# Block work of a normed token pair in another order, tiles turned one by one, scalings and weight blocks reordered at the kernel's start

## The reference

```python
x = x + 0.5 * swiglu(rmsnorm(x, norm_ffn1), w_ffn1_gate, w_ffn1_up, w_ffn1_down)
x = x + hybrid_mixer(rmsnorm(x, norm_mix), ...)      # windowed attention + gated linear attention
x = x + 0.5 * swiglu(rmsnorm(x, norm_ffn2), w_ffn2_gate, w_ffn2_up, w_ffn2_down)
return rmsnorm(x, norm_final)
# rmsnorm(x, g) = x * rsqrt(mean(x*x) + 1e-6) * g
# swiglu(h, wg, wu, wd) = (silu(h @ wg) * (h @ wu)) @ wd,   d_ff = 2816
```

## Time and profile before

| | us |
|---|---|
| median of three runs | 2178.97 (2178.81 to 2180.24) |
| the profiled execution | 2179.86 |
| its span | 2178.1 |
| TensorE busy (matmul) | 2140.5 |
| VectorE busy | 1500.4 |
| ScalarE busy | 842.4 |
| GpSimd busy | 330.0 |

### The profile page before, as it was taken

How to read it: one execution, slowest core, us unless ns; L and a number is a source line. 1 busy time by engine, 2 the same in 40 slices (tenths; PEclk the granted TensorE clock), 3 DMA queues, 4 the chain that set the end, 5 groups by cost and what they waited for, 6 DMA issues and landing times.

```text
span 2178.1 us, 32746 instructions
## 1 busy us (share of the span) xinstructions
PE 2140.5 (98%) x11950; PEld 1921.7 (88%) x11950; DVE 1500.4 (69%) x2702; ACT 842.4 (39%) x1688; POOL 330.0 (15%) x325
## 2 busy tenths in 40 slices
PE   6999999999999999999999999999999999999998
PEld 5999999999888888888888888899999999988887
DVE  7666677677666686988754557777776667757676
ACT  7233222222343355855543324422222322333343
POOL 7111111111100002201002334211111111100000
PEclk8999999999999999999999999999999999999999
DMA  4322222232586565433255872223322222387554
GB/s 127 101 82 91 91 88 88 97 106 91 186 287 208 174 209 163 132 103 108 79 150 167 285 240 95 65 88 97 100 97 82 91 91 87 113 285 256 176 187 166
DMA packets 245987, 301.17 MB, mean 138 GB/s; under 512 B 24194, under 2 KB 159746, under 8 KB 245828
## 3 DMA queue, kind: packets, MB, share of 16 engines
q1 hardware_dynamic: 237188, 285.97, 40.9%
q10 hardware_dynamic: 8640, 13.11, 1.7%
HBM read 206.29 MB, written 88.47 MB: 135 GB/s over the span
## 4 chain that ended last, share of the span: by engine, by line
PE 93%; DVE 3%; ACT 1%; issue 1%; DMA 1%; SPq 0%; POOL 0%; ACTq 0%; POOLq 0%; DVEq 0%
PE ps L2450 16%; PE ps L2446 12%; PE ps L2448 10%; PE ps L2449 10%; PE ps L2459 8%; PE ps L2458 8%; PE ps L2460 8%; PE ps L2372 4%; PE ps L2374 3%; PE ps L2373 3%; PE ps L2390 1%; PE ps L2392 1%; PE ps L2391 1%; PE ps L2643 1%; PE ps L2617 1%
## 5 line engine op out<-in xcount | busy, mean ns | idle before, releaser
L2450 PE MATMUL ps<-hs,w_lo 128*128 128x384 f32 (+1 forms) x992 | 305.2, 308 | 0.0
L2458 PE MATMUL ps<-w_hi,dh 128*128 128x512 f32 x770 | 300.2, 390 | 0.0
L2460 PE MATMUL ps<-w_hi,dh 128*128 128x512 f32 x770 | 299.7, 389 | 0.0
L1932 DVE TENSOR_TENSOR dh<-dr,dh 128x640 fp32r<-128x640 f32 x154 | 126.8, 823 | 161.7 <-ACT dh L1342 161.6
L2459 PE MATMUL ps<-w_lo,dh 128*128 128x512 f32 x610 | 237.3, 389 | 0.0
L2448 PE MATMUL ps<-hs,w_hi 128*128 128x384 f32 (+1 forms) x644 | 215.0, 334 | 4.9 <-DVE hs L1781 4.0
L1342 ACT CAST dh<-dr 128x640 fp32r<-128x640 f32 x154 | 112.2, 728 | 269.3 <-PE ps L2460 252.8
L2449 PE MATMUL ps<-hs,w_hi 128*128 128x384 f32 (+1 forms) x644 | 214.2, 333 | 0.0
L2446 PE MATMUL ps<-hs_first,w_hi 128*128 128x512 f32 x588 | 210.2, 391 | 0.0
L2446 PE MATMUL ps<-hs,w_hi 128*128 128x512 f32 x588 | 210.2, 391 | 0.0
L2449 PE MATMUL ps<-hq,w_hi 128*128 128x384 f32 x616 | 205.8, 334 | 0.0
(11 more groups left out here) (317 smaller groups left out, 4829.4 us busy)
## 6 DMA issues: line engine op xcount, KB each, us to landing
dr<-hid_mid SPq DMA_DIRECT2D x154, 320.0 KB, 3.2
w_raw<-in_w_ffn_down SPq DMA_DIRECT2D x176, 256.0 KB, 3.5
hid_mid<-st SPq DMA_DIRECT2D x88, 320.0 KB, 4.5
w_raw<-in_w_ffn_gate SPq DMA_DIRECT2D x44, 512.0 KB, 4.1
w_raw<-in_w_ffn_up SPq DMA_DIRECT2D x44, 512.0 KB, 3.9
hid_mid<-sg SPq DMA_DIRECT2D x66, 320.0 KB, 2.2
hq<-o_mid SPq DMA_DIRECT2D x70, 128.0 KB, 3.4
w_raw<-in_w_in SPq DMA_DIRECT2D x14, 512.0 KB, 5.5
```

The costliest lines, as they stand in the source:

```text
L1932: v.tensor_tensor(a_lo, DR[f][n % D_HID][:, :], a_hi.bitcast(F32), ALU.subtract).then_inc(W["a_lo"], 1)
L2450: last = mm(out, lo[:, k, :], b_hi, start=False, stop=k == 3, skip_group_check=True)
L2458: mm(out, hi, w_h, start=first and p in D_FRESH, stop=False, skip_group_check=True)
L2460: return mm(out, lo, w_h, start=False, stop=last, skip_group_check=True)
```

## The change

It has five parts.

- **VectorE's seven operations on a pair** go in the order t1, low GP1, t2, t4, low GP2, t3, low GP3. The two banks of the first tile have then been read for the last time after the fifth. `T_ORDER` gives ScalarE's and GpSimd's work on the sums the matching order t1, t2, t4, t3, in both feed-forward layers.
- **`norm_turn`** waits for each tile alone: the first for five operations of the pair before, the second for seven.
- **TensorE's list**: step (3,0) stands ahead of the turn of pair 4, not behind it.
- **VectorE's list**: the scaling of tile 3 goes between the fifth and the sixth operation of pair 0 (before: ahead of the first), and the blocks of pair 2 go ahead of `g_prepare(0, 1)` and `g_prepare(0, 2)` (before: behind them).
- **GpSimd** makes both roots of a pair at once for pairs 3 and 4 of the first layer.

```diff
         def xs_norm(f, n):
             return x_mixed(N_TILES[1][n]) if f else xs_first(n)
+
+        ROOT_PAIRS = 3
+        T_ORDER = ((GP5, 1), (GP6, 2), (GP4, 4), (GP7, 3))
         def norm_bank(f, i):
             return 4
...
                                         ).then_inc(N["root"], 1)
             def norm_roots(f, i):
+                if f == 0 and i >= ROOT_PAIRS:
+                    N, t = NFF[f], N_TILES[f][2 * i]
+                    both = slice(t, t + HT + 1, HT)
+                    pool.wait_ge(N["sum"], 2 * i + 2)
+                    nc.gpsimd.tensor_scalar(ssq[:, 0, both], ssq[:, 0, both], EPS, 1.0, ALU.add, ALU.mult).then_inc(N["root"], 2)
+                    pool.wait_ge(N["root"], 4 * i + 2)
+                    nc.gpsimd.tensor_tensor(rstd[:, 0, both], ssq[:, 0, both], expo[:, 0:2], ALU.pow).then_inc(N["root"], 2)
+                    return
                 for e in range(2):
                     root(2 * f, N_TILES[f][2 * i + e], 2 * i + e)
             def norm_t_lo(f, i):
                 pair = PAIR_ORDER[f][i]
-                for j, b in enumerate((GP5, GP6, GP7, GP4)):
+                for j, (b, m) in enumerate(T_ORDER):
                     pool.wait_ge(NFF[f]["hi"], 8 * i + 4 + j + 1)
-                    nc.gpsimd.tensor_tensor(h_piece(f, b, 1, pair), SUMS[f][j + 1][:, :], h_piece(f, b, 0, pair).bitcast(F32),
+                    nc.gpsimd.tensor_tensor(h_piece(f, b, 1, pair), SUMS[f][m][:, :], h_piece(f, b, 0, pair).bitcast(F32),
                                             ALU.subtract).then_inc(t_low[f], 1)
             def g_lo(f, s):
...
                 nc.scalar.copy(h_piece(f, GP3, 0, pair), ps[:, b + 3, :]).then_inc(N["hi"], 1)
                 nc.scalar.copy(h_piece(f, GP2, 0, pair), ps[:, b + 1, :]).then_inc(N["hi"], 1)
-            def norm_sums(f, i):
+            def norm_sums(f, i, part=slice(0, 4)):
                 N, pair = NFF[f], PAIR_ORDER[f][i]
-                for x, j, at in zip(SUMS[f][1:], (GP5, GP6, GP7, GP4), (1, 3, 4, 6)):
+                for (j, m), at in tuple(zip(T_ORDER, (1, 3, 4, 6)))[part]:
+                    x = SUMS[f][m]
                     act.wait_ge(N["lo"], 7 * i + at)
                     nc.scalar.copy(h_piece(f, j, 0, pair), x[:, :]).then_inc(N["hi"], 1)
...
             def norm_scale(f, n):
                 N, t = NFF[f], N_TILES[f][n]
-                dve.wait_ge(N["root"], 2 * n + 2)
+                dve.wait_ge(N["root"], 4 * (n // 2) + 4 if f == 0 and n // 2 >= ROOT_PAIRS else 2 * n + 2)
                 if f:
                     dve.wait_ge(gain_loaded, 16 * (2 * f + 1))
                     dve.wait_ge(x_spilled[n % 2], 16 * (HT + n // 2 + 1))
...
                 for e in range(2):
                     norm_scale(f, 2 * i + e)
-            def norm_blocks(f, i):
+            def norm_blocks(f, i, parts=(0, 1, 2)):
                 N, pair, b = NFF[f], PAIR_ORDER[f][i], norm_bank(f, i)
                 b12, t1, t2, t3, t4 = (x[:, :] for x in SUMS[f])
...
                     if i:
                         dve.wait_ge(t_low[f], 4 * (i - 1) + j)
-                t_free(1)
-                dve.wait_ge(N["hi"], 8 * i + 2)
-                v.tensor_tensor(t1, b12, ps[:, b, :], ALU.subtract).then_inc(N["lo"], 1)
-                lo(GP1, b)
-                t_free(2)
-                dve.wait_ge(N["hi"], 8 * i + 3)
-                dve.wait_ge(N["lo"], 7 * i + 1)
-                v.tensor_tensor(t2, ps[:, b + 3, :], t1, ALU.subtract).then_inc(N["lo"], 1)
-                t_free(3)
-                v.tensor_tensor(t3, ps[:, b + 3, :], b12, ALU.subtract).then_inc(N["lo"], 1)
-                lo(GP3, b + 3)
-                t_free(4)
-                dve.wait_ge(N["hi"], 8 * i + 4)
-                dve.wait_ge(N["lo"], 7 * i + 3)
-                v.tensor_tensor(t4, ps[:, b + 1, :], t2, ALU.subtract).then_inc(N["lo"], 1)
-                lo(GP2, b + 1)
+                if 0 in parts:
+                    t_free(1)
+                    dve.wait_ge(N["hi"], 8 * i + 2)
+                    v.tensor_tensor(t1, b12, ps[:, b, :], ALU.subtract).then_inc(N["lo"], 1)
+                    lo(GP1, b)
+                    t_free(2)
+                    dve.wait_ge(N["hi"], 8 * i + 3)
+                    dve.wait_ge(N["lo"], 7 * i + 1)
+                    v.tensor_tensor(t2, ps[:, b + 3, :], t1, ALU.subtract).then_inc(N["lo"], 1)
+                if 1 in parts:
+                    t_free(3)
+                    dve.wait_ge(N["hi"], 8 * i + 4)
+                    dve.wait_ge(N["lo"], 7 * i + 3)
+                    v.tensor_tensor(t4, ps[:, b + 1, :], t2, ALU.subtract).then_inc(N["lo"], 1)
+                    lo(GP2, b + 1)
+                if 2 in parts:
+                    t_free(4)
+                    v.tensor_tensor(t3, ps[:, b + 3, :], b12, ALU.subtract).then_inc(N["lo"], 1)
+                    lo(GP3, b + 3)
             def g_lo(f, s):
                 q, j = divmod(s, NP)
...
             v.memset(ones[:, :], 1.0).then_inc(const_set, 1)
             norm_scales(0, 0)
-            norm_scales(0, 1)
-            norm_blocks(0, 0)
+            norm_scale(0, 2)
+            norm_blocks(0, 0, (0, 1))
+            norm_scale(0, 3)
+            norm_blocks(0, 0, (2,))
             norm_scales(0, 2)
             g_lo(0, 0)
             norm_blocks(0, 1)
             norm_scales(0, 3)
+            norm_blocks(0, 2)
             g_prepare(0, 1)
             g_prepare(0, 2)
-            norm_blocks(0, 2)
             norm_scales(0, 4)
             norm_blocks(0, 3)
             for s in range(3):
...
                 for _ in range(n):
                     nc.tensor.transpose(ps[:, bank, 0:P], ident[:, :], ident[:, :])
-            def norm_turn(f, i):
+            def norm_turn(f, i, tiles=(0, 1)):
                 N, b = NFF[f], norm_bank(f, i)
-                if i:
-                    pe.wait_ge(N["lo"], 7 * i)
-                for e in range(2):
+                for e in tiles:
+                    if i:
+                        pe.wait_ge(N["lo"], 7 * i - (0 if e else 2))
                     pe.wait_ge(N["scaled"], 2 * i + e + 1)
                     for half in range(2):
                         for k in range(4):
...
                 a, b = PAIR_CUT[f][c]
                 pe.wait_ge(B["lo"], G_BLOCKS[f] + s + 1)
                 if q == 0:
-                    name, n, at = {GP1: (NFF[f]["lo"], 7, 2), GP6: (t_low[f], 4, 2), GP2: (NFF[f]["lo"], 7, 7),
-                                   GP7: (t_low[f], 4, 3), GP5: (t_low[f], 4, 1), GP4: (t_low[f], 4, 4),
-                                   GP3: (NFF[f]["lo"], 7, 5)}[j]
+                    name, n, at = {GP1: (NFF[f]["lo"], 7, 2), GP6: (t_low[f], 4, 2), GP2: (NFF[f]["lo"], 7, 5),
+                                   GP7: (t_low[f], 4, 4), GP5: (t_low[f], 4, 1), GP4: (t_low[f], 4, 3),
+                                   GP3: (NFF[f]["lo"], 7, 7)}[j]
                     pe.wait_ge(name, n * (b - 1) + at)
                 if j == GP1 and q:
                     if q % 2:
...
                 norm_turn(0, i)
             g_step(0, 0, 0)
             norm_turn(0, 3)
-            for j in range(1, 3):
+            for j in range(1, 4):
                 g_step(0, j, 0)
             norm_turn(0, 4)
-            for s, c in GORDER[3:]:
+            for s, c in GORDER[4:]:
                 g_step(0, s, c)
             def turn_mixed(t):
```

## The result

The changed kernel takes 2186.19 us (median of six executions, 2184.93 to 2188.30), the kernel before beside it 2179.45: a ratio of 1.0029, with a 95% interval of 1.0019 to 1.0039. That is 6.7 us slower, where 2.9 were forecast, and above the range. The profiled execution took 2186.48, its span is 2184.7 (before 2178.1, +6.6).

The account below looks back on a forecast made before the run. TensorE bounds the kernel (busy 2140.5 of 2178.1 us), so only its early stalls count: 3.6 us gained, then lost, then 2.8 late, taken as +2.9 in sum. From the median 2178.97 that gives 2181.9, range 2178.4 to 2183.9.

Parts of the forecast that it names:

- The chain: First 57 us: VectorE, ScalarE and back, with GpSimd beside it, end TensorE's wait for step (3,1), 2.7 to 3.1 late.
- costed at nothing: Joint roots, GP7's low, weight loads, second layer's turn of pair 4: no cost; cover gone 0.6 at most, either way.
- Part 2: Pair 1 and the first step: step (0,0) starts at 31.1 against 34.72, 3.6 us early.
- the first rival: VectorE-GpSimd meetings come out otherwise: one fewer held at 33.9, +1.8 (0.12); one more at 21.8, +4.1 (0.22).
- the near thing at 21.8: Low of block 0 comes as GpSimd changes instruction; if held, +1.2 on all that follows, +4.1 in sum, chance 0.22.
- Part 3: Before pair 3: GpSimd holds three moved weight operations, delaying ScalarE's copies; step (2,0) at 42.7 against 42.45, 3.6 us gone.
- Part 4: Step (3,0) ahead of pair 4's turn waits for an addition until 46.3; t1 of pair 4 2.8 us late.
- The slower rival: TensorE idling from 39.0 to 42.7 sets 1.2 GHz for steps (2,0), (3,0) and the turn: +6.3, 2185.3, chance 0.08.

Follow-up runs that it names:

- the filling: The changed kernel with 18 idle TensorE transposes of the identity between the tiles of the second layer's last turn: 2183.97 us, ratio 1.0019.

## Why the prediction was wrong

- **The chain was right.** Step (0,0) early (31.1 forecast, 32.01), the three held weight operations (1.75, 1.65, 1.65; measured 1.74, 1.74, 1.77), ScalarE idle until the difference is there (39.1; 40.13), step (2,0) behind idling (3.7; 3.40), step (3,0) at the addition, the turn of pair 4 behind it. By the Trainium skill, "SBUF — State Buffer", "Who interferes with whom", the third of them would be held beside GpSimd like the others; no row of before had it so, and the row at 38.33 agrees.
- **What failed is the size.** The span grew by 6.6 us where the sum had 2.9: 1.9 more at the beginning, and 1.8 in a part that was costed at nothing. The three places follow.
- **Part 2, what was mis-sized: the order of t2 and t4.** "Five operations" was costed at 0.60 each. In the order before, t3 and a low stood between t2 and t4; now t4 waits for t2's result. This costs 0.2 a pair, and 0.6 in pair 3, of which 0.4 has another, open cause: 1.4 us up to step (3,1), costed at nothing. It is also what let GpSimd in front of the first weight operation: the near thing of the first rival ("start within 0.1 us of each other") fell to GpSimd's side at 34.91 against 34.99, and to VectorE's (33.90 against 34.04) with the low ahead of t4.
- **Part 2, the near thing at 21.8.** The low of block 0 was held for 0.6 (1.29), half of what the rival had. With the 1.4 this is 2.0: step (3,1) at 61.68 where 59.6 to 59.9 was forecast, a difference of 1.8 to 2.1.
- **Part 3 named a link too many.** The high parts in front of pair 3's copies don't set t1 of pair 3; VectorE's own row does, and is as late (the run with the late high parts).
- **Part 4 was right in its mechanism and near in its size.** Its 2.8 us were the lateness of pair 4's t1 against the kernel before, 0.35 of it already in pair 3's (41.4 against 41.05), so some 2.4 for the step itself. Measured against the changed kernel, at step (3,1), it is 2.77; that this is the same figure is chance.
- **Costed at nothing: the second layer.** "0.6 at most" was +1.8. The idle time moved, as said, but a stretch at 1.2 GHz came with it that cost 2.6, against a gain of 0.8 that wasn't foreseen either. No term had a low clock there, though the earlier trace rows show that such stretches follow TensorE's idling; since it falls early or late from kernel to kernel, the sign of this term couldn't be had from the rows of before.
- **The slower rival** was half there. The clock fell for step (2,0) (0.50 in 44 to 47 us), and the wait for the addition hid it: 0.29 of waiting was left. In the profile of the kernel with one wait in layer 2, whose first layer is the same, it lasted past step (3,0) and cost 1.2; with the late high parts it cost 2.7.
- **The range** took one held operation as its upper end. The sum of small terms of one sign, each costed at nothing, went past it.

## What to carry to other kernels

Before an operation is moved up behind the one whose result it reads, on the same engine, count the wait, and put an independent one between the two. An engine that gains time early gives it back at the first row of another engine that it now meets, so follow the chain past the gain; and where TensorE's idle pieces are merged or moved, ask which steps then run at the low clock. Of a change made of several moves, undo each and all: here, counted behind the first t1, the three single runs gave back 2.7 us in sum, the three together 4.8, and a swap of two instructions that none of them touches 2.8.

## What the runs showed of the hardware that I had not expected

- **GpSimd holds a VectorE scaling that reads one SBUF tensor**, in place and with a per-partition factor: 2.56 us for 0.41, and GpSimd is held in turn where VectorE is first. The prediction spoke of two SBUF operands. The Trainium skill, "SBUF — State Buffer", "Who interferes with whom", names tensor_scalar among the operations that can do so, and the rows agree.
- **A VectorE operation that waits for its own engine's last result** starts 0.78 to 0.81 us behind it, where an independent one starts 0.60 behind (both of 512 columns). The Trainium skill, "VectorE: DVE Perf Modes", "The DRAIN you can't avoid", says of chained copies that a semaphore after each costs nothing extra. Here too an operation that only counts on a semaphore is followed after 0.60; what costs 0.2 us in these rows is waiting for the count of the operation right before, and the measurement decides.
- **Two kernels with a scratch tile of 64 bytes per partition take 14 us more.** In them the matmuls of 512 columns are slower throughout: of the changed kernel's 4828, one starts 229.3 ns behind the other on average, with the tile 233.1. The groups of TensorE by line and form, of the changed kernel and of the one with one more instruction:

```profile
L2475 PE MATMUL ps<-w_hi,dh 128*128 128x512 f32 x770 | 300.2, 390 | 0.0
```

```profile
L2477 PE MATMUL ps<-w_hi,dh 128*128 128x512 f32 x770 | 304.9, 396 | 0.0
```

  One and sixteen instructions cost the same (2200.25 and 2200.73), and the tile is what they share, with all later tiles of SBUF shifted by it; that the place of the tiles is the cause is argued, not isolated.
- **The granted clock falls in one of two places** of the second layer's beginning in all profiles but that with the filling, and the later one costs 1.3 to 2.6 us of the span. The spread of the executions of one kernel (3.4 us for the changed one) is of that size.
